# A three-block transformer kernel: the first z slot taken with the decay inputs, and the order of the last gate half and its stores

## The reference

```python
h = rms_norm_2(x, g_mix)
proj = h @ w_in
glu_a, glu_b, q, k, v, z, a_in, b_in, gate_a, gate_b = split_cols(proj, IN_SIZES)
c = glu_a * jax.nn.sigmoid(glu_b)
c = depthwise_conv(c, conv_dw_w) + conv_dw_b
...
g = -jnp.exp(a_log) * jax.nn.softplus(a_in + dt_bias)
beta = jax.nn.sigmoid(b_in)
o_fwd = gated_delta_rule(q, k, v, g[:, :, 0], beta[:, :, 0])
...
o = rms_norm_2(o_fwd + o_bwd, delta_norm_g) * jax.nn.silu(z)
...
x = x + jax.nn.sigmoid(rms_norm_2(x, g_pl) @ w_pl_gate) * pl
return rms_norm_2(x, g_final)
```

## Time and profile before

| what | us |
|---|---|
| three runs | 1198.54, 1201.29, 1202.06 |
| median | 1201.29 |
| profiled execution | 1202.13 |
| its span, first to last instruction | 1200.3 |
| TensorE busy | 1171.7 |
| VectorE busy | 839.7 |
| ScalarE busy | 701.5 |
| GpSimd busy | 324.8 |

### The profile page before, as it was taken

The page is one execution under the profiler, slowest core; times in us unless marked ns, Lnnn a source line. Parts: engine busy times, 40 slices in busy tenths (PEclk is TensorE's granted clock), DMA queues, the critical chain, the costliest instruction groups (busy, mean ns, idle before and its releaser), DMA issues.

```text
span 1200.3 us, 21345 instructions
## 1 busy us (share of the span) xinstructions
PE 1171.7 (98%) x8592; PEld 1088.5 (91%) x8592; DVE 839.7 (70%) x1519; ACT 701.5 (58%) x1181; POOL 324.8 (27%) x257
## 2 busy tenths in 40 slices
PE   8999999999999999999999999999999999999997
PEld 7777899998887799998899999999989989999886
DVE  6796588884685578885558787889954656555456
ACT  5466576663467676664466667667666445444344
POOL 1172300000028300000156666675555220000010
PEclk9999999999999999999979999999999999999999
DMA  7633355546553366555333332332223646555542
GB/s 286 252 141 141 125 210 210 184 181 216 176 178 139 124 244 211 202 188 211 141 137 118 132 111 104 140 109 102 105 72 108 226 176 222 209 186 201 203 154 81
DMA packets 31587, 199.74 MB, mean 166 GB/s; under 512 B 4289, under 2 KB 6481, under 8 KB 8706
## 3 DMA queue, kind: packets, MB, share of 16 engines
q1 hardware_dynamic: 29506, 189.27, 44.1%
q0 software_dynamic: 1840, 8.60, 1.9%
q10 hardware_dynamic: 144, 0.52, 0.1%
HBM read 197.33 MB, written 1.05 MB: 165 GB/s over the span
## 4 chain that ended last, share of the span: by engine, by line
PE 85%; DVE 7%; ACT 3%; issue 2%; POOL 1%; DMA 1%; SPq 0%; POOLq 0%; ACTq 0%; DVEq 0%
PE ps L1190 24%; PE ps L1192 23%; PE ps L1191 23%; PE ps L1567 2%; PE ps L1583 1%; PE ps L1344 1%; PE ps L1363 1%; DVE conv L2773 1%; PE ps L1331 1%; DVE wlo L2387 1%; PE ps L1215 1%; DVE ps L2842 1%; PE ps L1284 1%; PE ps L1197 1%; DVE x L2516 1%
## 5 line engine op out<-in xcount | busy, mean ns | idle before, releaser
L1190 PE MATMUL ps<-halves,whi 128*128 128x256 f32 x1472 | 410.7, 279 | 0.1
L1191 PE MATMUL ps<-halves,whi 128*128 128x256 f32 x1472 | 405.7, 276 | 0.0
L1192 PE MATMUL ps<-halves,wlo 128*128 128x256 f32 x1472 | 405.6, 276 | 0.0
L2387 DVE TENSOR_TENSOR wlo<-raw,whi 128x2048 fp32r<-128x2048 f32 (+1 forms) x133 | 300.7, 2263 | 116.1 <-ACT whi L1847 112.9
L1847 ACT ACTIVATE whi<-raw 128x2048 fp32r<-128x2048 f32 (+1 forms) x143 | 269.3, 1885 | 95.6 <-PE ps L1192 91.4
L1190 PEld LDWEIGHTS ps<-halves,whi 128*128 128x128 f32 x1472 | 283.3, 192 | 0.8 <-DVE halves L2981 0.5
L1192 PEld LDWEIGHTS ps<-halves,wlo 128*128 128x128 f32 x1472 | 283.4, 193 | 0.0
L1191 PEld LDWEIGHTS ps<-halves,whi 128*128 128x128 f32 x1472 | 283.4, 193 | 0.1
L1114 POOL TENSOR_TENSOR wlo<-raw,whi 128x1024 fp32r<-128x1024 f32 x72 | 172.4, 2404 | 54.5 <-ACT whi L1856 53.9
L1006 POOL TENSOR_TENSOR rstd<-sumsq,half_power 128x1 f32<-128x1 f32 x14 | 11.5, 823 | 573.9 <-ACT xn L1874 406.4
L1190 PE MATMUL ps<-whi,halves 128*128 128x512 f32 (+4 forms) x440 | 149.1, 339 | 3.6 <-DVE halves L2490 2.7
(11 more groups left out here) (337 smaller groups left out, 1849.3 us busy)
## 6 DMA issues: line engine op xcount, KB each, us to landing
raw<-in_stream SPq DMA_DIRECT2D x176, 1024.0 KB, 4.8
gain<-in_gains POOLq DMA_DIRECT2D x7, 512.0 KB, 5.6
bias<-in_rel POOLq DMA_DIRECT2D x1, 1536.0 KB, 8.5
raw<-in_stream SPq DMA_DIRECT2D x2, 648.0 KB, 7.9
cst<-in_consts POOLq DMA_DIRECT2D x1, 1280.5 KB, 8.9
raw<-in_stream SPq DMA_DIRECT2D x2, 528.0 KB, 4.2
x<-in_x SPq DMA_DIRECT2D x2, 512.0 KB, 4.6
out<-xn SPq DMA_DIRECT2D x4, 256.0 KB, 2.4
```

The costliest lines, as they stand in the source:

```text
L1190: nc.tensor.matmul(out, a_hi, b_hi, start=start, stop=False)
L1191: nc.tensor.matmul(out, a_hi, b_lo, start=False, stop=False)
L1192: return nc.tensor.matmul(out, a_lo, b_hi, start=False, stop=stop)
L2387: dve.tensor_tensor(used(wlo, n), used(raw, n), used(whi, n).bitcast(F32), ALU.subtract)\
```

## The change

The slot "ab" goes. In its place stand two slots, ("z_decay", 0) and ("z_decay", 1): the first and the last 512 rows of 288 columns, the 256 of ("z", 0) and the 32 of a_in and b_in. `first_z_and_decay_products(t)` makes 24 matmuls of 288 columns for each tile into bank 4 + t. The slot ("z", 0) leaves round 1; the slots behind it move up, and round 4 is left with three. z's tanh (ScalarE) and product (VectorE), `first_z`, stand at tick 7 of round 0, and `level_turn(0)` on TensorE waits for the product, since it writes bank 4. The splits of the following slots move: the whole of ("z_decay", 0) is VectorE's, that of ("z_decay", 1) GpSimd's ahead of the second tile's deviation, ("qk", 0) is split behind the norm, ("v", 0) is rounded by ScalarE behind the norm, and ScalarE's second half of glu 0 goes from tick 1 to tick 2 of round 0.

At the end the tanh of unit (0, 1, 0) goes ahead of the first tile's scaling, on VectorE the work of that unit too, and the two second halves of the output are stored by ScalarE's queue.

```diff
         down(f"down{layer}", ("ffn_w_down", layer), FT)
-    plan.append(("narrow", "ab", ("w_in_2", 0), 6144, 32))
+    rows_major("z_decay", ("w_in_2", 0), [(5120, 2 * P), (6144, 32)])
...
     out = [(("conv_out", i), "w_conv_out_2", 2 * i * P, (2 * i + 1) * P) for i in range(KT // 2)]
-    other = [glu[0:2], [z[0]] + glu[2:4], [glu[4], z[1]], [z[2], glu[5], z[3]], [glu[6], gates[0]],
+    other = [glu[0:2], glu[2:4] + [z[1]], [glu[4], z[2]], [glu[5], z[3], gates[0]], [glu[6]],
...
-MIX_SLOTS = [("ab", -1, 0)] + [(slot[0], r, 2 * i) for r, slots in enumerate(ROUNDS) for i, slot in enumerate(slots)] \
+MIX_SLOTS = [(("z", 0), -1, 0)] + [(slot[0], r, 2 * i) for r, slots in enumerate(ROUNDS) for i, slot in enumerate(slots)] \
...
     return slot_at(r, i - 1) if i else slot_at(r - 1, TICKS - 1)
...
+FIRST_Z_AT = (0, 7)
...
         ident_loaded, consts_loaded, params_loaded, rows_loaded, bias_loaded, gain_loaded, consts2_loaded, \
-            params2_loaded, p_loaded, stored = [ctx.enter_context(nc.semaphore(name)) for name in (
+            params2_loaded, p_loaded, stored, second_stored = [ctx.enter_context(nc.semaphore(name)) for name in (
                 "ident_loaded", "consts_loaded", "params_loaded", "rows_loaded", "bias_loaded", "gain_loaded",
-                "consts2_loaded", "params2_loaded", "p_loaded", "stored")]
+                "consts2_loaded", "params2_loaded", "p_loaded", "stored", "second_stored")]
...
             for t in range(TT):
-                for half in range(2):
-                    c = slice(half * 512, (half + 1) * 512)
-                    sp.wait_ge(*(S["gate_tanh_made"].at(("final", t)) if half else S["normed"].at((NORMS - 1, t))))
-                    sp.dma_start(dram["out"][t * P:(t + 1) * P, c], xn[:, t, c]).then_inc(stored, 16)
-            sp.wait_ge(stored, 16 * 2 * TT)
+                sp.wait_ge(*S["normed"].at((NORMS - 1, t)))
+                sp.dma_start(dram["out"][t * P:(t + 1) * P, 0:512], xn[:, t, 0:512]).then_inc(stored, 16)
+            sp.wait_ge(stored, 16 * TT)
...
                 if t == 0:
-                    split_shared(("qk", 0))
+                    n = slot_of[("z_decay", 1)]
+                    pool.wait_ge(*S["weights_high"].at((n, 1)))
+                    pool.tensor_tensor(used(wlo, n), used(raw, n), used(whi, n).bitcast(F32), ALU.subtract)\
+                        .then_inc(*S["pool_weights_low"].one((n, 1)))
...
             pool.memset(glu_in[:, :, :], 0.0).then_inc(*S["glu_cleared"].one())
+            split_shared(("qk", 0))
...
-            def ab_products(t):
...
-                n = slot_of["ab"]
-                if t == 0:
-                    wait_low(pe, n)
-                wh, wl = used(whi, n), used(wlo, n)
-                for kt in range(KT):
-                    if kt % 4 == 0:
-                        wait_split(5, t, (kt // 4,))
-                    last = three(ps[:, 3, t * 32:(t + 1) * 32], xhi[:, kt, t * P:(t + 1) * P], xlo[:, kt, t * P:(t + 1) * P],
-                                 wh[:, kt, :], wl[:, kt, :], kt == 0, kt == KT - 1)
-                if t:
-                    last.then_inc(*S["weights_used"].one(n))
+            def first_z_and_decay_products(t):
...
+                for half in range(2):
+                    n = slot_of[("z_decay", half)]
+                    if t == 0:
+                        wait_low(pe, n)
+                    wait_split(5, t, (half,))
+                    wh, wl = used(whi, n), used(wlo, n)
+                    for i in range(4):
+                        kt = 4 * half + i
+                        last = three(ps[:, 4 + t, 0:Z_DECAY], xhi[:, kt, t * P:(t + 1) * P], xlo[:, kt, t * P:(t + 1) * P],
+                                     in_order(wh[:, i, :]), in_order(wl[:, i, :]), kt == 0, kt == KT - 1)
+                    if t:
+                        last.then_inc(*S["weights_used"].one(n))
...
                 pe.wait_ge(*S["inverse_begun"].at(h))
+                if h == 0:
+                    pe.wait_ge(*S["tanh_used"].at(("z", 0)))
...
                 round_turned(5 if k == 4 else k, [(1, 0), (1, 1)])
+                if k == 4:
+                    split(last + 4)
...
                     .then_inc(*S["p_high"].one())
...
+            def first_z():
...
+                act.wait_ge(*S["weights_used"].at(slot_of[("z_decay", 1)]))
+                act.wait_ge(*tanh_free(TANH_BEFORE[("z", 0)]))
+                act.activation(tanh[:, TANH_OF[("z", 0)], :].rearrange("p (t c) -> p t c", t=2), ps[:, 4:6, 0:2 * P], ACT.Tanh,
+                               scale=0.5).then_inc(*S["tanh_made"].one(("z", 0)))
...
                         evacuate(finished_slot(r, i))
+                    if (r, i) == FIRST_Z_AT:
+                        first_z()
...
                         conv_tanh(("v", r // 2))
-                    if slot_at(r, i):
+                    if (r, i) == (0, 2):
+                        split_half(slot_of[slot_at(0, 1)] + AHEAD, 1)
+                    if slot_at(r, i) and (r, i) != (0, 1):
...
                     .then_inc(*S["gate_tanh_made"].one(("final", t)))
+                act.wait_ge(*S["gate_tanh_made"].at(("final", t)))
+                act.dma_start(dram["out"][t * P:(t + 1) * P, 512:D], xn[:, t, 512:D]).then_inc(second_stored, 16)
...
             gate_tanhs((0, 0, None))
+            gate_tanhs((0, 1, 0))
             last_half(0)
-            for c in range(2):
-                gate_tanhs((0, 1, c))
+            gate_tanhs((0, 1, 1))
             last_half(1)
+            act.wait_ge(second_stored, 16 * TT)
...
                     scale_x(0)
+                    split(last + 2)
...
                 lows(after, [(1, 0), (1, 1)])
+                if k == 4:
+                    split(last + 3)
...
-                dve.wait_ge(*S["weights_used"].at(slot_of["ab"]))
+                dve.wait_ge(*S["weights_used"].at(slot_of[("z_decay", 1)]))
                 dve.wait_ge(params2_loaded, 16)
-                link(dve.tensor_copy(ab[:, 0, :, :], ps[:, 3, 0:64].rearrange("p (t c) -> p t c", t=2)))
+                link(dve.tensor_copy(ab[:, 0, :, :], ps[:, 4:6, 2 * P:Z_DECAY]))
...
                     .then_inc(*S["rows_low"].one("mixer"))
...
+            def first_z():
...
+                dve.wait_ge(*S["tanh_made"].at(("z", 0)))
+                dve.scalar_tensor_tensor(xn[:, :, 0:TOK], tanh[:, TANH_OF[("z", 0)], :].rearrange("p (t c) -> p t c", t=2), 1.0,
+                                         ps[:, 4:6, 0:2 * P], ALU.add, ALU.mult).then_inc(*S["tanh_used"].one(("z", 0)))
...
             add_squares((0, 0, None), sumsq_5[:, 0:1], sumsq[:, 0:1]).then_inc(*S["x_added"].one((8, 0, 1)))
-            last_half(0)
...
             dve.wait_ge(*S["squared"].at((8, 1)))
-            link(add_squares((0, 1, 0), sumsq_5[:, 1:2], pl_sq[:, 1:2]))
+            second_sum = add_squares((0, 1, 0), sumsq_5[:, 1:2], pl_sq[:, 1:2])
+            last_half(0)
+            link(second_sum)
```

More of the change, by code:

```diff
@@ L175, in pack_stream @@
                 out[n].reshape(P, KT, 2 * P)[:] = evens_first(out[n].reshape(P, KT, 2 * P))
-        elif kind == "narrow":
-            a, c = args
-            out[n].reshape(P, KT, 256)[:, :, 0:c] = w[:, a:a + c].reshape(KT, P, c).transpose(1, 0, 2)
         elif kind == "down":
@@ L547 @@
 AB_SPINS = (6, 2)
+Z_DECAY = 2 * P + 32
 END_SPINS = (5, 8)
@@ L944, in channel_tile @@
             return m * HEADS + key[1] if key[0] == "qk" else 2 * HEADS + 2 * key[1] + m
-        POOL_SLOTS = [slot_of[key] + AHEAD for key, r, tick in MIX_SLOTS if 0 <= r < len(ROUNDS)]
+        POOL_SLOTS = [slot_of[key] + AHEAD for key, r, tick in MIX_SLOTS if 0 <= r < len(ROUNDS)] + [slot_of[("z_decay", 1)]]
         OUT_SHARED = {layer: [(f"{layer}_out", OUT_SLOT[2]), (f"{layer}_out", OUT_SLOT[3]), (f"up{li}", 0)]
@@ L1777, in _ @@
                 turn_norm(5, t)
-                ab_products(t)
+                first_z_and_decay_products(t)
                 if t == 0:
@@ L3032, in _ @@
             decay_inputs()
-            split(slot_of["ab"] + AHEAD)
+            split(slot_of[("z_decay", 1)] + AHEAD)
             for r in range(len(ROUNDS)):
```

4 lines of the change are left out of this document (2 added, 2 removed).

## The result

| | before | after |
|---|---|---|
| median | 1201.29 us | 1205.75 us (1204.67 to 1206.75) |
| profiled execution, its span | 1202.13, 1200.3 us | 1206.56, 1204.6 us |

The ratio is 1.0036, with a 95% interval of 1.0018 to 1.0053. The forecast was 1192.6 us with a range of 1189.8 to 1196.8: the kernel became slower by 4.5 us where it should have become faster by 8.7, and no rival of the prediction ends there by its mechanism.

What follows compares the result with a forecast made beforehand. TensorE, busy 98% of the span, was taken as the bound; -3.76 - 3.3 - 1.9 + 0.9 - 0.75 - 0.3 = -9.1 us gave 1193.0 or 1192.2, forecast 1192.6 us, range 1189.8 to 1196.8.

Steps and rivals of the forecast that it cites:

- The norm stage, first tile: Before ("qk", 0): rounding 0.8 us later but hidden; GpSimd's split 0, at most +0.6; ("qk", 0) near 12.2 us.
- GpSimd is locked out: Rival in the norm stage: GpSimd's slow split, 0.6 us, delays the deviation behind it; 1193.2 to 1193.8 us; chance 10%.
- The sign that the prediction named for being wrong: Norm stage: second tile's normalization still waiting for GpSimd as long, or idle time ahead of 597.3 over 1.3 us.
- The decay path: Round 0, ("qk", 0)'s evacuation behind the decay functions: TensorE waits 1.45 us for gated, 0.57 before by the same reckoning; +0.9 us.
- The chance of 7% for this path: Rival in round 0: evacuation and taps behind the decay functions wait two or three us more; 1194.6 to 1195.6; 7%.
- The clock: Norm stage, 600 to 615: granted clock stays at its upper level, so ("qk", 0)'s first products take 2.0 us; -1.9 us.
- Behind it all of TensorE is queued: Round 0 behind the gated tile's wait: TensorE's work follows without further change; 0 us.
- a slower case by the clock: Rival in the short rounds: gaps bring the clock to its lower level in one of them; over 1205 us; chance 2%.
- Round 4: Round 4 with one slot less becomes as long as round 6, 32.90 us: -3.76 us, lower bound 3.0.
- Z's tanh and product: Tick 7 of round 0, behind VectorE's cross: the new wait in `level_turn(0)` is met early; 0, at most +0.7 us.
- The earlier quarter tanh: At the end, the last unit starts at 1192.6 and not 1193.42, and all behind it comes earlier; -0.75 us.
- The two queues: At the end, two queues issue the last two stores, saving one issue; -0.3 us, bounds 0 and -0.4.

Runs made afterwards that it cites:

- the two collisions taken out and one queue: Changed kernel with GpSimd's splits waiting for the first tile's normalization and for the first gated tile, all output stores on SP's queue: 1195.62 us, ratio 0.9952.
- both of GpSimd's waits: Changed kernel with GpSimd's splits held until the first tile's normalization is written and until the gated tile of ("qk", 0) is written: 1197.70 us, ratio 0.9973.
- the kernel with one of them: Changed kernel with only GpSimd's half split at tick 2 of round 0 waiting for the gated tile of ("qk", 0): 1201.79 us, ratio 0.9999.

## Why the prediction was wrong

**The failed steps** are the two that priced a neighbour of GpSimd's splits, and the stretch behind the second one, which was put at nothing. The sum was -9.1 us and the profiled executions differ by +4.3, so it is off by 13.4. By the table 2.3 of these are the norm stage, 3.5 the way to the gated tile, 4.5 the clock behind it, 1.2 round 4, 0.4 the two queues, 0.3 round 1, and 1.1 stand ahead of the change.

*The norm stage, first tile.* The prediction took GpSimd's moved split, saw that it would stand near 594 beside VectorE's normalization, and charged what that does to GpSimd: up to 0.6 us. It never charged VectorE. The rival "GpSimd is locked out" has the same fault, one direction only. VectorE's second half took 3.1 us and not 0.75 and TensorE waited 2.00 us; without the collision the step is right: 12.49 us to ("qk", 0), forecast 12.2. The 0.8 us of later rounding were hidden, as said. The rule cited there (the Trainium skill, "SBUF — State Buffer", section "SBUF: two separate sides") says that whichever of the two starts first holds the ports for its whole instruction. This case's rows agree in both directions. GpSimd held VectorE: 3.78 for 1.41 us, and 4.46 for 0.81. VectorE held GpSimd: in the kernel before, the half split at 612.04 took 4.21 us and not 2.36 behind VectorE's split from 611.73 to 614.02. The sign that the prediction named for being wrong came too: idle time ahead of the first products over 1.3 us (2.00 and 1.23).

*The decay path.* The forecast was a wait of 1.45 us ahead of the gated tile, from a chain of 5.73 us measured in a place where GpSimd happened to be idle. Up to the chain it was right: the evacuation was to begin 6.3 us after ("qk", 0) (613.6 - 607.3) and began 6.30 after it (616.99 - 610.69). The chain then took 9.36 us and not 5.73. With GpSimd's idleness restored the wait is 1.07. With the splits back to back it is 4.78: a duration was carried over without what ran beside it. The chance of 7% for this path, and its price of 2 or 3 us, missed the 4.51 us that the clock adds behind the wait.

*The clock.* The forecast that it would stay at its upper level from 600 to 615 came true in the profile (1.00), and the rows are gone. That it was worth -1.9 us was too simple. The low stretch came back from 626 to 635, behind the wait, where it cost 4.51, and the step "Behind it all of TensorE is queued" put that at nothing. Nor did it stay up in the norm stage each time: behind the 2.00 us wait it fell there in two of the profiled executions (0.57 from 597 to 605, 0.53 from 600 to 607), with the same products of 288 columns. And the clock in these stages is not a property of the kernel alone: over 23 executions of the kernel before, timed beside the second group of experiments, the mean granted clock ranged from 0.991 to 0.996 and the time from 1203.3 to 1198.2. The prediction named a slower case by the clock, but put it into the rounds from 4 on, where it stayed at 1.00 (755 to 890), and not behind a new wait. That the wider slot costs little holds: its first 24 products took 3.0 us (600.66 to 603.67), as forecast, where the narrow ones took 2.7 (597.32 to 599.99).

*Round 4.* The mechanism was right, the term too big: -2.58 for -3.76, and less than the 3.0 that was given as its lower bound (the range used 1.6, for which the prediction gives no reason). "The same kinds of slots" was false: round 6 has a gates slot in third place, which ScalarE alone evacuates, round 4 a glu slot. With a gates slot there it measured 32.84, so the term lost 1.1 to 1.2 us to that.

*Z's tanh and product*, 0 with at most +0.7, show as +0.30 in round 1 (34.13 for 33.83): VectorE's product of z (0.68 us) stands ahead of the taps there, and TensorE's first wait for `prod` is 0.98 us for 0.39. No run tests this alone, and the slots of round 1 changed as well.

*The end.* The earlier quarter tanh: -0.74 for -0.75, right. The two queues: +0.13 for -0.3, and with the DMA issue ahead of the last tanh 0.35 us worse than one queue. The prediction saw that issue and gave it 0.1; it is 0.18. The rule beside it (the Trainium skill, "DMA: Bandwidth & Descriptors", section "Issuing engines are not separate DMA queues") allowed one issue at most, and the runs gave less than nothing: the landings, at the median 2.9 us for 2.4, took that back.

With the two collisions taken out and one queue, the kernel takes 1195.6 us, inside the forecast's range and 3.0 above its value. By landmarks round 4 is 1.15 us of these, the stretch from gated to round 1 0.4 (19.01 for 18.60, with the splits held back), the norm stage 0.3, z 0.3 and the end 0.1; the rest is of the size by which executions differ. That this kernel ends inside the range says nothing for the prediction, which was made for the kernel with the collisions in it.

## What to carry to other kernels

When an edit moves a split or any other tensor_tensor on GpSimd, list VectorE's instructions with two SBUF inputs that now run beside it, and charge the collision to both engines: a rarely busy engine can hold up the path for a whole instruction, twice in a row when its queue is full. A duration or a chain read from a profile holds only with its neighbours, so look at what the other engines did in that gap before carrying it over. Price a new wait of TensorE with what the clock may do behind it (4.5 us behind 4.8 here), and compare kernels by stretches between landmarks, since executions differ in the clock by as much as the change is worth.

## What the runs showed of the hardware that was not expected

With three of GpSimd's splits back to back, VectorE got in between two of them for one instruction only. The two gated instructions of the changed kernel took 1977 and 2558 ns (392 and 486 before), each until a split had ended. The view by tile of the changed kernel (min/median/max ns):

```profile
L2850 DVE SCALAR_TENSOR_TENSOR gated<-tanh,conv x2: 1977/2268/2558, 621.8 to 623.7; 128x256 f32<-128x256 f32 x2
```

VectorE's taps with one PSUM and one SBUF input were not held up: of the eight in the changed kernel the first two ran ahead of the splits and the others beside them, and each took 473 to 482 ns. And the length of a wait alone does not tell what the clock does behind it: idle waits of 1.06 to 1.08 us ahead of the gated tile were followed by a low clock in the four profiled executions with both of GpSimd's waits and without spins (20.14 to 20.19 us to round 1), while one of 1.07 us in the kernel with one of them was not (19.02).
